# Twelve of the second network's 56 projection tiles per layer, made as fp32 products between the steps of attention and RWKV

## What is computed

```
u = rmsnorm(x, ln1_w[l])
proj = u @ w_in[l]
rw = token_shift(proj[..., :RWKV_COLS], rwkv_mu[l])
...
g_a, g_b, g_c = [jax.nn.sigmoid(c) for c in cols[11:14]]
o_a = rwkv7_mixer(...)
o_b = nsa_mixer(...)
o_c = swa_sink_mixer(...)
merged = g_a * (o_a @ w_br_a[l]) + g_b * (o_b @ w_br_b[l]) + g_c * (o_c @ w_br_c[l])
x = x + merged @ w_out[l]
```

## Time and profile before

| | us |
|---|---|
| Median of 3 runs | 4839.38 (4836.96 to 4841.16) |
| The profiled execution | 4839.24 |
| its span in the trace | 4837.4 |
| `ProjectIn`, first to last block, layer 0 | about 161 (28 blocks) |
| Attention and RWKV, layer 0 | 2116 to 2399 |
| Attention and RWKV, layer 1 | 3566 to 3840 |

### The profile page before, as it was taken

The page is one execution under the profiler, slowest core; times in us unless marked ns, Lnnn a source line. Parts: engine busy times, 40 slices in busy tenths (PEclk is TensorE's granted clock), DMA queues, the critical chain, the costliest instruction groups (busy, mean ns, idle before and its releaser), DMA issues.

```text
span 4837.4 us, 72126 instructions
## 1 busy us (share of the span) xinstructions
PE 4549.6 (94%) x29770; PEld 4088.8 (85%) x29770; DVE 1591.8 (33%) x3003; ACT 1731.8 (36%) x2728; POOL 2710.3 (56%) x1314
## 2 busy tenths in 40 slices
PE   7999999999989898998889999999998889999998
PEld 5777777878778798876888999998877888999998
DVE  2211222032023331434568311114434568311114
ACT  3222322232133243443133444444442233444443
POOL 2443233444345277751176888887750266888886
PEclk9999999999999999987799999999988799999999
DMA  6623355222223144440043355555440043355554
GB/s 252 241 100 94 104 235 203 93 87 96 87 105 122 50 163 163 167 151 1 11 151 114 122 182 182 182 182 188 178 148 1 27 149 101 139 182 182 182 182 154
DMA packets 100148, 659.23 MB, mean 136 GB/s; under 512 B 10464, under 2 KB 16864, under 8 KB 22368
## 3 DMA queue, kind: packets, MB, share of 16 engines
q1 hardware_dynamic: 90000, 638.46, 36.4%
q10 hardware_dynamic: 9936, 17.73, 1.4%
HBM read 646.71 MB, written 9.44 MB: 136 GB/s over the span
## 4 chain that ended last, share of the span: by engine, by line
PE 87%; DVE 8%; ACT 2%; POOL 2%; issue 1%; DMA 1%; SPq 0%; ACTq 0%; DVEq 0%; POOLq 0%
PE ps L247 23%; PE ps L248 23%; PE ps L249 23%; PE ps L2591 3%; PE ps L2387 3%; POOL ring_rest L263 1%; PE ps L402 1%; PE ps L1445 1%; PE ps L1476 1%; DVE arena L2111 1%; PE ps L1798 1%; PE ps L1845 1%; PE ps L1008 1%; DMA arena<-in_mod_weights 1%; DVE arena L2793 1%
## 5 line engine op out<-in xcount | busy, mean ns | idle before, releaser
L263 POOL TENSOR_TENSOR ring_rest<-ring,rounded 128x1024 fp32r<-128x1024 f32 x992 | 2416.0, 2458 | 1577.6 <-ACT rounded L235 1324.8
L247 PE MATMUL ps<-part,rounded 128*128 128x256 f32 (+1 forms) x5760 | 1839.9, 319 | 100.6 <-POOL ring_rest L263 30.2
L248 PE MATMUL ps<-part,rounded 128*128 128x256 f32 (+1 forms) x5760 | 1826.1, 317 | 0.0
L249 PE MATMUL ps<-part,ring_rest 128*128 128x256 f32 (+1 forms) x5760 | 1824.9, 317 | 0.0
L247 PEld LDWEIGHTS ps<-part,rounded 128*128 128x128 f32 x5760 | 1109.8, 193 | 207.3 <-issue 33.4
L249 PEld LDWEIGHTS ps<-part,ring_rest 128*128 128x128 f32 x5760 | 1108.9, 193 | 69.2
L248 PEld LDWEIGHTS ps<-part,rounded 128*128 128x128 f32 x5760 | 1109.8, 193 | 66.9
L235 ACT ACTIVATE rounded<-ring 128x1024 fp32r<-128x1024 f32 x528 | 528.7, 1050 | 736.9 <-PE ps L249 727.2
L2748 ACT ACTIVATE rounded<-ring 128x1024 fp32r<-128x1024 f32 x464 | 489.0, 1054 | 318.4 <-DMA ring<-in_weights 314.0
L247 PE MATMUL ps<-x_parts,rounded 128*128 128x256 f32 x1984 | 564.3, 284 | 4.8 <-DVE x_parts L580 3.4
L248 PE MATMUL ps<-x_parts,rounded 128*128 128x256 f32 x1984 | 562.7, 284 | 0.0
(11 more groups left out here) (341 smaller groups left out, 4624.5 us busy)
## 6 DMA issues: line engine op xcount, KB each, us to landing
ring<-in_weights SPq DMA_DIRECT2D x528, 1024.0 KB, 4.8
arena<-in_mod_weights SPq DMA_DIRECT2D x72, 1024.0 KB, 7.8
held<-arena ACTq DMA_DIRECT2D x20, 256.0 KB, 5.5
arena<-held SPq DMA_DIRECT2D x20, 256.0 KB, 4.1
arena<-bias_scratch ACTq DMA_DIRECT2D x2, 2048.0 KB, 9.2
bias_scratch<-arena ACTq DMA_DIRECT2D x1, 3072.0 KB, 32.3
x<-in_x SPq DMA_DIRECT2D x1, 2048.0 KB, 9.9
arena<-in_keys ACTq DMA_DIRECT2D x2, 1024.0 KB, 5.1
```

The source lines that it names most:

```text
L247: mm(out, w[0], a[0], start=start, stop=False)
L248: mm(out, w[0], a[1], start=False, stop=False)
L249: return mm(out, w[1], a[0], start=False, stop=stop)
L263: eng.tensor_tensor(c.ring_rest[:, slot, half], c.ring[:, slot, half], c.rounded[:, (self.s0 + r) % ROUNDED, half].bitcast(F32), ALU.subtr ...
```

## The change

`ProjectIn` keeps 22 blocks. The other 6 of each layer (tiles 44 to 55: the last four tiles of one gate and all eight of another) move behind the compression weights in the stream and become whole blocks of `Attention`. A new class `GatesAhead` makes them: DVE adds the two parts of the input to one fp32 input at the start of `ProjectIn`; PE multiplies the weight tiles from the ring with it, 96 fp32 matmuls per layer, in bank 6; ACT copies each finished block out and, at t = 1 of `Rwkv`, applies the sigmoid to all twelve tiles. A table says how many matmuls stand at which point: 16 after the compression, 4 in each of the units 0 to 7, and in `Rwkv` for each t 8 at the masks and one before each `x` of the levels 1 to 4; at t = 1 also 12 before L1820, 2 before L1829 and 2 before L1837. To free bank 6, the sums of `values` use bank 7 alone, with a wait for the copy of the sum before; the outputs' first half uses bank 4; `squares` uses bank 7, so `bonus` waits for DVE's read of it and moves from level 3 to level 4.

```diff
-          "in2": 28, "cmp1": 4, "cmp2": 1, "rwkv": 1, "branch": 6, "out2": 4, "wq": 8,
+          "in2": 28 - AHEAD, "ahead": AHEAD, "cmp1": 4, "cmp2": 1, "rwkv": 1, "branch": 6, "out2": 4, "wq": 8,
...
     def dve(self, dve, link):
+        dve.wait_ge(self.chip.stage_done, self.index)
+        self.next.ahead.sum(dve, self.u)
         dve.wait_ge(self.kept.sem, self.kept.at(T_NQ // 2))
...
+def ahead_points():
+
+    yield "compressed", 16
+    for u in range(16):
+        yield ("unit", u), 4 if u < 8 else 0
+    for t in range(NT):
+        yield (t, "masks"), 16 - 2 * (LEVELS - 1)
+        for lv in range(1, LEVELS):
+            for g in range(2):
+                yield (t, "level", lv, g), 1
+        yield (t, "inverse"), 12 * t
+        yield (t, "values"), 2 * t
+        yield (t, "weights"), 2 * t
...
+    def products(self, pe, point):
+        c = self.chip
+        for n in range(*self.count[point]):
+            j, i = divmod(n, TPB)
+            e, k = divmod(i, KD)
+            slot, count = self.stage.arrival(self.first + j)
+            if i == 0:
+                if j == 0:
+                    pe.wait_ge(self.ready.sem, self.ready.at(1))
+                else:
+                    pe.wait_ge(self.kept.sem, self.kept.at(j))
+                pe.wait_ge(c.loaded[slot], count)
+            last = self.nc.tensor.matmul(c.ps[:, self.BANK, e * N:(e + 1) * N], c.ring[:, slot, i, :], self.whole[:, k, :],
+                                         start=k == 0, stop=k == KD - 1)
+            if i == TPB - 1:
+                last.then_inc(c.block_done, 1)
...
+    def keep(self, act, point):
+        first, end = (n // TPB for n in self.count[point])
+        for j in range(first, end):
+            act.wait_ge(self.chip.block_done, self.stage.block_count(self.first + j))
+            to = self.to[:, 2 * j:2 * j + 2, :].rearrange("p a n -> p (a n)")
+            self.nc.scalar.activation(to, self.chip.ps[:, self.BANK, :], ACT.Copy).then_inc(self.kept.sem, 1)
+
+    def gate(self, act):
+        act.wait_ge(self.kept.sem, self.kept.at(AHEAD))
+        for h in range(2):
+            part = self.to[:, h * AHEAD:(h + 1) * AHEAD, :]
+            self.nc.scalar.activation(part, part, ACT.Sigmoid).then_inc(self.kept.sem, 1)
...
-            if n >= 2:
-                pe.wait_ge(self.sum_kept.sem, self.sum_kept.at(n - 1))
+            if n:
+                pe.wait_ge(self.sum_kept.sem, self.sum_kept.at(n))
...
-                last = nc.tensor.matmul(ps[:, 6 + n % 2, :], v, weights.rearrange("p i t -> p (i t)"),
+                last = nc.tensor.matmul(ps[:, 7, :], v, weights.rearrange("p i t -> p (i t)"),
...
         def squares(t):
             pe.wait_ge(s["gn_sq"].sem, s["gn_sq"].at(t + 1))
-            half_sums(6, self.gn[0]).then_inc(s["gn_var"].sem, 1)
+            half_sums(7, self.gn[0]).then_inc(s["gn_var"].sem, 1)
 
         def bonus(t):
             pe.wait_ge(s["rk"].sem, s["rk"].at(1))
-            pe.wait_ge(s["gn_centred"].sem, s["gn_centred"].at(t + 1))
+            pe.wait_ge(s["gn_in"].sem, s["gn_in"].at(t + 1))
...
+            pe.wait_ge(s["l_kept"].sem, s["l_kept"].at(8 * t + 3))
+            ahead.products(pe, (t, "masks"))
             pe.wait_ge(s["l_kept"].sem, s["l_kept"].at(8 * t + 8))
...
-                    if lv == 3:
+                    if lv == 4:
                         bonus(0)
...
+            ahead.products(pe, (t, "inverse"))
             pe.wait_ge(s["d_done"].sem, s["d_done"].at(2 * self.LEVELS * (t + 1)))
```

84 lines of the change are left out of this document (71 added, 13 removed).

## The result

| | before | after |
|---|---|---|
| median, us | 4838.19 (4836.96 to 4841.16, 4 runs) | 4776.09 (4772.84 to 4777.70, 4 runs) |
| profiled execution, us | 4839.24 | 4772.84 |
| its span, us | 4837.4 | 4771.0 |

The ratio is 0.987, with a 95% interval of 0.9853 to 0.9887: 1.3% faster. The profiled executions differ by 66.4 us; the sum had 59.1 and 4780.1 us.

A forecast was written before the change was run, and what follows sets the result against it. PE was taken as the bound, holding 87% of the chain. The terms -69.1 + 1.8 - 4.3 + 1.5 - 1 + 1.2 + 9.2 + 1.6 gave -59.1, from 4839.24 to 4780.1 us; range 4766 to 4808.

The forecast's parts named there:

- the likeliest case: Whole kernel: the forecast band of 4774 to 4786 us, given a chance of 0.45.
- `ProjectIn`, -69.1: In `ProjectIn`, six blocks of 5.76 us per layer come off the path: -69.1 us in two layers.
- 16 products after the compression, +1.8: Before the first scores, 6.9 us of products overrun PE's waits by 0.7 and 1.1 us: +1.8 us.
- Units 0 to 7, -7.6 and +3.3: Attention's units 0 to 7: 37.9 us with products at full clock, -7.6 us in layer 0 and +3.3 in layer 1.
- the rival of a fall in part of the units: Units 0 to 3 stay at low clock, 17.6 us per affected layer: 4787 to 4820 us, chance 0.27.
- the row of the expert stage: Cost of one product, from 160 like matmuls in the expert stage: 0.432 us at 2.4 GHz, about 0.86 at 1.2.
- One bank for the values' sums, +1.5: Last values, units 14 and 15: PE waits for the first sum's copy, 0.75 us each layer, +1.5 us.
- Masks, -1, and levels, +1.2: RWKV: masks gain 1 us from full clock over four places; levels overrun 0.3 us per t and layer, +1.2.
- After the levels, +9.2: RWKV, t = 1: twelve products cost +4.3 us, two and two +0.3, together +9.2 us in two layers.
- Second `bonus`, +1.6: After `squares`, PE waits for DVE's spread, 0.8 us each layer, and PE bounds the branches behind: +1.6 us.
- A clock that is low throughout: Half clock in the 16 products, units, masks and the twelve: +108 us, 4888; from 4820 up, chance 0.06.
- the point of decision at 59 us: The change turns slower once over 59 of 108 us, counted at full clock, run at 1.2 GHz.

The follow-up runs named there:

- version with ten blocks: Ten blocks instead of six, four products in each of 16 units, two ahead of each chunk wait, sigmoids behind second root, against the changed kernel: 4753.11 us.

## Why the prediction was right

The forecast was the likeliest case, and the total came 7 us lower. The mechanism is right in its main steps: the removed blocks come off in full, and the products keep the clock up in most of the units and cost there one for one. That the total is so near is partly luck: units, the rest of Attention and the group norm were together 8.1 us dearer than the sum had, and the steps and chunks of t = 1 were 11.2 us cheaper. Point by point:

- **`ProjectIn`, -69.1.** The first token-shift product (L1706, now L1802) started at 2082.90 instead of 2117.62, 34.7 us earlier. Right, though this start moved by up to 2.5 us between profiles with the same instructions ahead of it (2082.90 to 2085.42).
- **16 products after the compression, +1.8.** In layer 0 PE went on at once and the scores started 0.8 us later than the removed blocks alone give (said: 0.7). In layer 1 the term was below 0: there the token-shift products ran at full clock and PE came 3.1 us sooner to the compression, but DVE did not, and 1.58 us of the wait stayed. Counted from the first token-shift product, the first scores came only 0.4 us sooner, and the wait cost in the next term.
- **Units 0 to 7, -7.6 and +3.3.** Measured -6.8 and +7.3. The stretch near 38 us at 1.00 came in layer 0 (38.67); in layer 1 it was 41.92, with PEclk at 0.50 for some 7 us. Right in mechanism, and the step that failed in layer 1 is "in PE's wait of 6 us, which the 16 products now fill": they fill 7.1 us of what was 8.7 there. What lowered the clock is only in part what the step says: with the wait filled and no products in the units it fell within 5 us all the same. By the rival of a fall in part of the units this is its small form, 3.3 us instead of 17.6. The products took 7.10 us for 16, 0.44 each, and 0.416 to 0.43 where they were removed: the row of the expert stage held, not four passes of 0.120.
- **One bank for the values' sums, +1.5.** The waits are 0.77 us. The bank changes alone cost 1.0 us per layer in Attention; the changed kernel had 2.5 and 1.0, the more in layer 0 from a longer time at 0.50 in the last values.
- **Masks, -1, and levels, +1.2.** `x` (L1900) starts 7.31 us after the first decayed product of t = 0 and L1798 started 6.98 after it before: +0.33, said +0.3. Both terms together, per layer at t = 0: -0.6 and -0.3, said +0.05. At t = 0 the levels hid their products almost wholly; the sum had asked 0.3 us for them.
- **After the levels, +9.2.** The stretch with the twelve: +4.2 and +3.4, said 4.35 with masks and levels. The match is a sum of three: -1.8 and -2.6 that come with the bank changes, +1.8 with the products at masks and levels, and +4.2 with the twelve. The step that failed is the one behind it: "Two and two, 0.86 us each, against 0.69 and 0.78" with +0.3, and nothing for the chunks. Measured -5.2 and -5.4. The prediction had seen that a full clock there gives something back, priced it from L1829 alone at 1.3 us, and kept it for the range. It did not ask how far the full clock would carry: it lasted through the first chunk, which took 4.1 us instead of 6.6. The late 16 products account for 3.7 and 3.8 us of the gain; the other 1.6 came without them, in L1829 and the outputs. This is the largest error of the sum, 11.2 us in two layers, and why the total was lower.
- **Second `bonus`, +1.6.** The wait is 0.88 us, but "PE bounds the branches behind it" was wrong: PE waited 11.22 us for DVE in the same stretch before the change, and with the bank changes alone the stretch was no longer than before. The number came out (+1.4 and +1.5 us per layer against 0.8) because a second step was wrong too, "the table for the later square root is loaded while ACT waits": ACT was rounding a block at that time, and the load came behind it and ahead of the root. Before the change there was no second load at all, since the root's table stayed in from the first. Moving the sigmoids gave 2.7 us per layer back.
- **Rivals.** A clock that is low throughout was 0.06, with the point of decision at 59 us. The version with ten blocks shows such a stretch, though this change has none: the same kind of mix stayed at 1.2 GHz for 43 us in each layer.

## What to carry to other kernels

Where PE is full at half clock, a stretch is not at its limit by the count of its matmuls: look for PEclk before costing an added matmul, since full-row matmuls between small ones may make the stretch shorter than it was without them. Cost the clock of the stretch behind an edit as well as of the stretch that holds it. And where a table of ACT is used twice with idle time between, look at what a new function in that idle time throws out.

## What the runs showed of the hardware that was not expected

- The clock stayed at 1.00 through units 0 to 7 in nine layers without a wait before them, one with two products in each unit (32.02 us) and eight with four (38.67 us); without any, the clock fell within 5 us of the same scores, though it had been full when they began. With four it fell as well in the version with ten blocks (46.79 us), with PE busy throughout.
- A wait of 1.58 us before the first scores was followed by a fall to 0.50 of 6.9 us in both profiles of the changed kernel, and waits of 1.57 to 1.60 us by falls in five further layers; with the wait filled or absent and six blocks it did not come there, in nine layers.
- The same order of instructions ran four chunks at 5.35 us or at 10.15 us each, by whether the clock came back after a fall in waits of 0.85, 0.69 and 0.78 us ahead of them. PE's busy share was 100% in both. What decides whether it comes back was not found; that it need not fall there was shown.
- Elementwise steps of DVE with two operands in SBUF took 0.69 us alone and 2.77 us beside POOL, so 1.4 us more of waiting for a root cost 4 us more of DVE time, and 2.7 us in all reached the end.
